# A two-layer diffusion trunk: the latent-attention scores as three products of split queries and keys

## The reference

```
def softmax_attention(q, k, v):
    scale = QK_C ** -0.5                      # QK_C = 64 + 32 = 96
    def block(qb):
        s = jnp.einsum('bqhd,bkhd->bhqk', qb, k).astype(F32) * scale
        p = jax.nn.softmax(s, axis=-1)
        return jnp.einsum('bhqk,bkhe->bqhe', p.astype(v.dtype), v)
    return sweep_query_blocks(block, q)
```

## Time and profile before

| | |
|---|---|
| median of 3 runs | 2151.04 us (2149.22 to 2155.87) |
| the profiled execution | 2148.85 us |
| its span, first to last instruction | 2146.9 us |
| TensorE busy | 1921.9 us (90%) |
| VectorE busy | 1419.8 us (66%) |
| ScalarE busy | 1030.7 us (48%) |
| mean granted TensorE clock | 0.938 of full |

### The profile page before, as it was taken

One profiled execution on the slowest core, in us unless ns is written; L12 is line 12 of the kernel. 1 busy time (PEld: TensorE's weight loads), 2 busy tenths in 40 slices (PEclk: granted clock), 3 DMA queues, 4 the chain that ended last, 5 costly groups with the idle time before them and its releaser, 6 DMA issues.

```text
span 2146.9 us, 28619 instructions
## 1 busy us (share of the span) xinstructions
PE 1921.9 (90%) x11283; PEld 1730.4 (81%) x11283; DVE 1419.8 (66%) x2030; ACT 1030.7 (48%) x1387; POOL 278.2 (13%) x411
## 2 busy tenths in 40 slices
PE   5989789897999999997996889885599999999994
PEld 2987677797999999997995777784488888888883
DVE  4476884436665566535657774334589888888887
ACT  3236686513221211223246676314477777777772
POOL 0073410100111111000255310001000000000002
PEclk9999899798999999998997899797799999999997
DMA  8125200022554555321120000003789999999996
GB/s 319 59 85 201 79 1 1 20 99 99 176 176 159 177 176 179 117 84 45 54 91 25 1 1 1 1 1 154 306 343 384 403 391 402 390 401 398 383 386 229
DMA packets 115910, 375.64 MB, mean 175 GB/s; under 512 B 8640, under 2 KB 66400, under 8 KB 89408
## 3 DMA queue, kind: packets, MB, share of 16 engines
q1 hardware_dynamic: 94448, 303.50, 37.7%
q0 software_dynamic: 14240, 51.49, 7.1%
q10 hardware_dynamic: 7088, 18.81, 2.2%
HBM read 347.13 MB, written 26.64 MB: 174 GB/s over the span
## 4 chain that ended last, share of the span: by engine, by line
PE 75%; DVE 14%; ACT 5%; issue 3%; DMA 2%; SPq 1%; POOL 1%; ACTq 0%; DVEq 0%; POOLq 0%
PE PS L1957 31%; PE PS L1898 25%; PE PS L1644 5%; PE PS L1937 5%; PE PS L1760 5%; PE PS L1732 3%; ACT E L795 2%; DVE NM L1143 2%; DVE KCn L1115 1%; DMA rows_of_slots<-HTM,SLI 1%; DMA araw<-in_w_ada_head 1%; DVE split L1387 1%; DVE SS L1098 1%; ACT PT L802 1%; DVE NT__177 L1438 1%
## 5 line engine op out<-in xcount | busy, mean ns | idle before, releaser
L1957 PE MATMUL PS<-H,split 128*128 128x320 f32 x2688 | 402.9, 312 | 14.4 <-DVE H L1578 12.5
L1957 PEld LDWEIGHTS PS<-H,split 128*128 128x128 f32 x2688 | 400.9, 191 | 16.3 <-issue 15.0
L968 ACT CAST split<-raw 128x2048 fp32r<-128x2048 f32 (+2 forms) x64 | 112.8, 1763 | 269.1 <-PE PS L1957 230.4
L1387 DVE TENSOR_TENSOR split<-raw,split 128x2048 fp32r<-128x2048 f32 (+2 forms) x64 | 138.0, 2161 | 127.5 <-ACT split L968 127.5
L1305 DVE TENSOR_TENSOR split<-raw,split 128x2048 fp32r<-128x2048 f32 x82 | 187.0, 2290 | 51.6 <-ACT split L923 51.5
L1305 DVE TENSOR_TENSOR msplit<-raw,msplit 128x2048 fp32r<-128x2048 f32 x82 | 187.9, 2292 | 31.9 <-ACT msplit L923 31.8
L1898 PE MATMUL PS<-split,HT 128*128 128x512 f32 x816 | 196.8, 397 | 5.5 <-DVE HT L1284 5.5
L1898 PE MATMUL PS<-msplit,HT 128*128 128x512 f32 x816 | 190.6, 389 | 0.0
L923 ACT CAST msplit<-raw 128x2048 fp32r<-128x2048 f32 x82 | 156.9, 1914 | 63.8 <-PE PS L1898 63.8
L923 ACT CAST split<-raw 128x2048 fp32r<-128x2048 f32 x82 | 157.2, 1917 | 61.6 <-PE PS L1898 45.8
L1644 PE MATMUL PS<-split,H 128*128 128x384 f32 (+1 forms) x960 | 170.6, 339 | 14.0 <-DVE split L1387 10.7
(11 more groups left out here) (299 smaller groups left out, 2881.4 us busy)
## 6 DMA issues: line engine op xcount, KB each, us to landing
raw<-in_moe_w_gate SPq DMA_DIRECT2D x55, 1024.0 KB, 7.0
raw<-in_moe_w_down SPq DMA_DIRECT2D x55, 1024.0 KB, 7.8
raw<-in_moe_w_up SPq DMA_DIRECT2D x54, 1024.0 KB, 7.2
DOTW<-in_w_ada_rows POOLq DMA_DIRECT2D x56, 512.0 KB, 4.3
raw<-in_w_ada_head SPq DMA_DIRECT2D x16, 1024.0 KB, 7.2
mraw<-in_moe_w_up SPq DMA_DIRECT2D x14, 1024.0 KB, 7.3
mraw<-in_moe_w_gate SPq DMA_DIRECT2D x13, 1024.0 KB, 7.1
mraw<-in_moe_w_down SPq DMA_DIRECT2D x13, 1024.0 KB, 8.1
```

Source lines behind the costliest of these rows:

```text
L968: A.copy(split[u % 2][:, 0, 0:w], src[:, 0:w]).then_inc(S["split_hi"], 1)
L1387: V.tensor_tensor(split[u % 2][:, 1, 0:w], src[:, 0:w], split[u % 2][:, 0, 0:w].bitcast(f32), ALU.subtract).then_inc(S["split_lo"], 1)
L1957: ins = T.matmul(PS[:, 4 * (u % 2) + 2 * c + hf, 0:HALF], W[:, w, k, c * P:(c + 1) * P], A[:, a, k, hf * HALF:(hf + 1) * HALF], start=(k = ...
```

## The change

`LT` becomes two planes in float32r. ScalarE's copy in `turn_out` writes plane 0, the rounded values. After the scaling of item k-1's output, VectorE waits for that copy and writes the remainder of the group, PSUM minus plane 0, into plane 1; it signals this on a new semaphore, `turn_lo`. TensorE waits for it before it turns the next group (the bank is read by both) and before a head's first score. A score is now three products into the same place: rounded queries by rounded keys, rounded queries by the keys' remainder, and the queries' remainder by rounded keys.

```diff
--- before.py
+++ after.py
@@ -249,7 +249,7 @@
         KT = [at(f"KT{s}", [P, 2, KT_TILES * P], OFF_SPLIT + s * 16384 + 5120, f32r) for s in range(2)]
         QS = [at(f"QS{s}", [P, NT, 2, 4, DA], OFF_SPLIT + s * 16384 + 11264) for s in range(2)]
 
-        LT = [at(f"LT{s}", [QK, (NT + KT_TILES) * P], OFF_SPLIT + s * 16384) for s in range(2)]
+        LT = [at(f"LT{s}", [QK, 2, (NT + KT_TILES) * P], OFF_SPLIT + s * 16384, f32r) for s in range(2)]
         ACTB = at("ACTB", [P, 2, KC, TOK], OFF_R, f32r)
         SG = at("SG", [P, 2, TOK], OFF_R + 61440)
         AT = at("AT", [P, 2, TOK], OFF_R + 66560)
@@ -342,7 +342,7 @@
                  "setA_free setB_free proj_ready proj_free "
                  "nsq_ready nsq_used root_ready x_root eps_ready normed roped cache_loaded stores "
                  "ct_turned ct_hi ct_lo lat_ready lat_q lat_k subln_gained "
-                 "q_stacked k_stacked turned turn_out scored max_ready exp_ready w_ready pt_ready pt_out o_ready o_stored "
+                 "q_stacked k_stacked turned turn_out turn_lo scored max_ready exp_ready w_ready pt_ready pt_out o_ready o_stored "
                  "subln_sq subln_sum subln_root subln_done mix_turned mix_hi mix_lo conv_hi conv_lo act_ready act_hi act_lo "
                  "router_loaded router_hi router_lo logits_ready logits_out top_ready top_exp gates_ready "
                  "crow_in crow_ready dot_used dots zeroed tables_ready h_rows_ready rows_turned rows_out mask_ready rank_ready slots_ready owners_ready scattered "
@@ -746,7 +746,7 @@
                     dst = (QT[s] if g < 3 else KT[s])[:, :, :].rearrange("p c n -> p (c n)")
                     first, end = 512 * (g % 3), (2 * TOK if g < 3 else 12 * P)
                 else:
-                    dst, first, end = LT[s], 512 * g, 11 * P
+                    dst, first, end = LT[s][:, 0, :], 512 * g, 11 * P
                 n = min(512, end - first)
                 A.copy(dst[:, first:first + n], PS[0:dst.shape[0], 1 if h else 7, 0:n]).then_inc(S["turn_out"], 1)
 
@@ -1185,6 +1185,13 @@
                     modulation_out(1)
                     gain(0, 1)
                     dve.wait_ge(S["mod_ready"], 2)
+                if (hg := groups_at(k, 0)) is not None and hg[0] >= HEADS:
+                    h, g = hg
+                    n = groups_before(h) + g + 1
+                    first, end = 512 * g, min(512 * (g + 1), (NT + KT_TILES) * P)
+                    dve.wait_ge(S["turn_out"], l * TURNS + n)
+                    V.tensor_tensor(LT[h % 2][:, 1, first:end], PS[0:QK, 1, 0:end - first],
+                                    LT[h % 2][:, 0, first:end].bitcast(f32), ALU.subtract).then_inc(S["turn_lo"], 1)
 
                 if k == 0:
                     latents_scale(NT - 1, 1)
@@ -1671,6 +1678,8 @@
                 n = l * TURNS + groups_before(h) + g
                 if h or g:
                     pe.wait_ge(S["turn_out"], n)
+                if h > HEADS or h == HEADS and g:
+                    pe.wait_ge(S["turn_lo"], l * 3 * HEADS + 3 * (h - HEADS) + g)
                 if h < HEADS:
                     stack, tiles, first = (QS[h % 2], NT, 4 * g) if g < 3 else (KS, KT_TILES, 4 * (g - 3))
                     blocks = [stack[:, j % tiles, j // tiles, :, :].rearrange("p a d -> p (a d)")
@@ -1722,14 +1731,20 @@
                     pe.wait_ge(S["exp_ready"], l * SCORES + n - 1)
                 if j % NT == 0 and c == 0:
                     pe.wait_ge(S["turn_out"], l * TURNS + groups_before(h + 1))
+                    if h >= HEADS:
+                        pe.wait_ge(S["turn_lo"], l * 3 * HEADS + 3 * (h - HEADS + 1))
                 width = HALF if t else P
                 for hf in range(2 if t else 1):
                     first = P + hf * HALF if t else 0
+                    out = PS[:, 2 + 2 * (n % 2) + hf, 0:width]
                     if h < HEADS:
-                        q, k_ = QT[s][:, c, t * P:(t + 1) * P], KT[s][:, c, first:first + width]
+                        ins = T.matmul(out, QT[s][:, c, t * P:(t + 1) * P], KT[s][:, c, first:first + width],
+                                       start=True, stop=True)
                     else:
-                        q, k_ = LT[s][:, t * P:(t + 1) * P], LT[s][:, TOK + first:TOK + first + width]
-                    ins = T.matmul(PS[:, 2 + 2 * (n % 2) + hf, 0:width], q, k_, start=True, stop=True)
+                        for q, k_ in ((0, 0), (0, 1), (1, 0)):
+                            ins = T.matmul(out, LT[s][:, q, t * P:(t + 1) * P],
+                                           LT[s][:, k_, TOK + first:TOK + first + width],
+                                           start=(q == k_), stop=(q == 1))
                 ins.then_inc(S["scored"], 1)
 
             turn_group(0, KT_TILES - 1)
```

## The result

The changed kernel takes 2173.93 us (median of 13 runs, 2163.81 to 2193.21); the kernel before, on the same chip, 2150.13 (13 runs, 2144.58 to 2164.85). The ratio is 1.0108 [1.0081, 1.0135], some 23 us slower. The forecast was 2165, with 2159 to 2171 for the forecast's own bounds and a wider range that took in part of the rival with the falling clock. The sign held, and so did the wait for the subtraction as the main cause; the loss was 1.6 times the forecast 14, because the clock, which the forecast left alone, fell as well.

What follows compares the result with a forecast made beforehand. TensorE was taken as near its limit, with added subtractions making it wait. Head terms summed to 7.1 us a layer, 14.2 in both, on 2148.85: 2163, plus 2.2 to the timed median, 2165; forecast's own range 2159 to 2171.

Steps and rivals of the forecast that it cites:

- Bound: Second kind's heads: TensorE near its limit, busy 76 of 80 us; the chain of waits leaves it twice per 13.47 us head.
- TensorE's part: Scores: big ones 0.88 us instead of 1.08, small ones 0.64 instead of about 0.23; 4.7 us saved in both layers.
- VectorE's part: 18 subtractions added per layer, 685 ns for 512 elements, 552 for 384; TensorE released after 0.73 or 0.59 us.
- A plain head: Second kind's head without extra steps, such as head 6: 14.1 us from first score to the next's for 13.47, +0.7.
- Heads 7 and 8: Heads with 0.54 us sums of squares between output and subtraction, one holding up a late-ending subtraction: +1.0 and +1.2 us.
- Head 9: Head with the two square-root table loads and the root's small steps ahead of a subtraction on VectorE: +2.3 us.
- First kind's last head: Its items turn the first new head's groups while VectorE is busy 3.86 of 4 us; three subtractions nearly all on the path: +1.5.
- Head 10: Second kind's head after the table loads' head, priced like a plain head: +0.7 us.
- the clock falls: Rival: TensorE's waits in each head lower its granted clock, 14 us more, 2179 us; chance 0.12.
- Head 11: Last head, which turns nothing; two cheaper big scores on the path: -0.3 us.
- cheaper scores win: Rival: subtractions fit VectorE's idle half, turning and values cover their waits, 4.7 us go: 2146 us; chance 0.12.
- only the ends of heads cost: Rival: waits inside a head are absorbed, three fifths of the loss stay, about 2157 us; chance 0.08.

Runs made afterwards that it cites:

- e1: Changed kernel without VectorE's subtraction and both waits for it, all three products of a score reading plane 0; 0.996 of the kernel before.
- e5: The changed kernel run again, unedited; 1.0115 of the kernel before.
- e9: The kernel before, unchanged, profiled once more on another chip; 2149.8 us.
- e4: Changed kernel plus idle TensorE transposes of the identity, four before a head's first score, five before its fourth and fifth; 1.0081 of the kernel before.
- e11: e6 plus five idle transposes ahead of each score of a head's last two items; 0.9991 of the kernel before.
- e6: Changed kernel with blocks turned keys first, so a head's first score needs two groups and only its third the last; 1.0022 of the kernel before.
- e10: Changed kernel with every subtraction done twice, same result; 1.0347 of the kernel before.
- e2: Changed kernel with one float32 product of plane 0 per score again, subtraction and both waits kept; 1.0104 of the kernel before.
- e8: Changed kernel with each group of the second kind's heads turned, copied and subtracted one item earlier; 1.0057 of the kernel before.
- e3: e1 with VectorE's subtraction back in place, both inputs from plane 0 in SBUF, nobody waiting for it; 1.0001 of the kernel before.
- e7: e6 with no VectorE subtraction: ScalarE copies groups to SBUF, GpSimd writes rounded values and remainder; 0.9957 of the kernel before, 2148.75 us.

## Why the prediction was right, and where it fell short

- **Bound**: right in the main. New waits of TensorE were paid in full, but of the 4.7 us of cheaper products e1's trace shows only 2.5 on the path, which leaves TensorE twice in each head.
- **TensorE's part**: the big score right (forecast 0.88 us, seen 0.88 to 0.90). The small score was over-priced, 0.64 for 0.37 us: the 0.53 us of two products in the earlier trace rows held more than their two issues. It made the gain too small by 0.27 x 6 = 1.6 us a layer. The Trainium skill ("TensorE: Matmul & The Clock Gate", section "Back-to-back issue gap") gives about 56 ns for 128 columns as the gap of an isolated product and about 81 ns in a stream of weight loads and products. e1's 120 ns, for the rounded format, agrees with neither and lies nearer to them than my 0.21 us.
- **VectorE's part**: 686 and 545 ns against 685 and 552, right, and so is the wait of TensorE for it. The release was priced too short: from a subtraction's start to TensorE's 0.84 us in the chain, not 0.73, and that comes three times a head.
- **A plain head**: 14.38 us for the forecast 14.1 to 14.2. The step that failed is the one I had put in brackets, the way round through the next output, called 0.15 us shorter than the way through maximum and exponential. With 0.84 for each wait, 0.28 instead of 0.20 for the scaling and 0.10 ahead of it, that way is the longer one, and it is the way that the chains of heads 6 and 7 take.
- **Heads 7 and 8**: forecast +1.0 and +1.2, measured +1.49 and +1.65; the same two terms, and both sums of squares lie in the loop.
- **Head 9**: +2.3 forecast, +2.05 in layer 0, where the clock falls only near its end; with it low earlier, +3.0 (e5) or +5.1 (layer 1). Its 16.29 us before aren't firm either: e9 has 15.16.
- **First kind's last head**: +1.5 forecast, +1.6 and +3.2 from the first product of the latent projection to the first new score. That stretch has falls of the clock of its own, and e4 has -1.0 and +3.1 there, so the head's share is not shown.
- **Head 10**: the step that failed most. +0.7 was forecast, +5.5 measured, and e4, with the fall kept short, has +0.97. The forecast gave the clock nothing. The rival "the clock falls" had a chance of 0.12 and was placed in every head; it came true in one place a layer, behind the table loads, where TensorE's busy time fell to 2.30 and then 2.19 of 4 us, and not in the plain heads ahead of it (clock 1.00 from 324 to 384 us). So one of the prediction's own signs of being wrong, a clock at half inside the stretch, came true. The rule of the Trainium skill that the prediction cites for this rival ("TensorE: Matmul & The Clock Gate", section "A second HAM failure mode: psum-queue depth-cycling"), told there of a bf16 kernel, is that micro-idles between groups of matmuls can make the clock oscillate. The runs agree with it, each in its direction: e4 (14.44 for 19.00 us), e11 (13.90 for e6's 16.51) and e10 (falls in most heads).
- **Head 11**: -0.3 forecast; -4.6 in the first profile and -0.7 in e5, by the clock alone.

Adding up: with the clock's falls kept as short as before (e4's trace) the attention parts are 15.7 us longer, for 14.2 forecast. The ratios say 23 to 25 us for the change and 17.5 for e4: of the 9 to 11 us above the forecast some 7 are the clock's, the rest the loop's larger terms. In the first profile itself: first kind +1.6 and +3.2, new heads +11.4 and +14.4, last heads -4.6 twice, the part behind -1.1, the parts ahead +1.2, which makes the 21.4 us of the spans. That the first profile comes so near the forecast is in part luck: without the last heads' full clock it would be 9 us longer.

Of the signs named ahead, the subtraction's time and count, the waits for VectorE and the 0.9 us of six score records came; heads 14.1 to 14.6 us apart came for plain ones (14.38), not for heads 7 and 8 (15.0 and 15.1).

The rival that cheaper scores win fell with e2 and the chain: turning and values, which were to cover the wait, stand behind it. That only the ends of heads cost is half true: e6, which takes the wait at the end alone away, removes 0.54 us of the 0.91 to 1.49 added in the first two distances. (Its price of 2157 us adds to the profiled 2148.85; from the median, as the forecast does, it is 2159.5.)

## What to carry to other kernels

When an operation is put between two engines that hand a single buffer to and fro, cost the loop that it closes, with what stands ahead of it in its engine's order; its duration beside that engine's idle share says little. A slower engine that nobody waits for (GpSimd, 1.9 us a group) can be better than a faster one in the loop (VectorE, 0.7), if the consumer's order leaves it the time. Where TensorE's waits gather near a place at which it already idles, look at the granted clock of each 4 us and price a stretch at 1.2 GHz; moving the waits apart (e8) or idle work in them (e4) tells within one run whether it is the clock. And compare a variant with the kernel before part by part in the traces: a ratio of whole times can hold 10 us of a place that the edit never touched.

## What the runs showed that I had not expected

- Idle transposes made a kernel faster (1.0081 for 1.0108 and 1.0115, and 0.9991 for 1.0022).
- Doubling 36 instructions of 0.55 to 0.69 us cost 50 us, twice their own 23 us; at full clock a head paid only for the instructions themselves.
- Waits of 1.14, 0.88 and 0.45 us a head left the clock full; a single 1.81 us behind the table loads' idle times was followed by 12 us at 1.2 GHz. Without any wait for the subtraction (e3) those idle times were followed by 8 us.
- A subtraction with both inputs in SBUF took 1.06 to 1.21 us instead of 0.69 four times, each time with GpSimd multiplying beside it; with one input in PSUM, beside the same multiplications, it never did.
- VectorE's release of TensorE took 0.14 us where ScalarE's took 0.04 to 0.05.
- GpSimd's 1.27 us subtractions beside VectorE left the maximum where it was, 0.82 us in the mean of 144 in e7 as in the kernel before.
